# One channel group of the large convolution on GpSimd, 25 more table rows in the large projection, two items of the last stage at other places

## What is computed

```python
def conformer_conv(u, w_dw, b_dw, ln_g, ln_b):          # CONV_K = 31, CONV_W = 512
    a, gt = jnp.split(u, 2, axis=-1)
    h = a * jax.nn.sigmoid(gt)
    hp = jnp.pad(h, ((0, 0), (CONV_K - 1, 0), (0, 0)))
    h = lax.conv_general_dilated(hp, w_dw[:, None, :].astype(h.dtype), window_strides=(1,), padding='VALID',
                                 dimension_numbers=('NWC', 'WIO', 'NWC'), feature_group_count=CONV_W) + b_dw
    return jax.nn.silu(layer_norm(h, ln_g, ln_b))

def peer_ffn(x, w_q, sub_k1, sub_k2, u_tab, v_tab):
    ...
    top_s, top_j = lax.top_k(cand_s, PEER_TOPK)          # 8 heads x 16 experts for each token
    idx = jnp.take_along_axis(cand_i, top_j, axis=-1)
    g = jax.nn.softmax(top_s, axis=-1).astype(x.dtype)
    ...
    def one_chunk(args):                                 # 128 tokens
        xb, ib, gb = args
        act = jax.nn.gelu(jnp.einsum('cd,ced->ce', xb, u_tab[ib]), approximate=False)
        return jnp.einsum('ce,ced->cd', gb * act, v_tab[ib])
```

## Time and profile before

| what | us |
|---|---|
| median of 3 runs | 3703.0 (3701.9 to 3706.6) |
| the profiled execution, its own time | 3718.67 |
| its span | 3716.9 |
| large projection, in the trace | 500 to 843 |
| attention and merge of the 768 tokens | 843 to about 1760 |
| last stage: blocks of u | 1905 to 2893 |
| last stage: blocks of v | 2893 to 3604 |
| last table row | ends 3681 |

### The profile page before, as it was taken

The page is one execution under the profiler, slowest core; times in us unless marked ns, Lnnn a source line. Parts: engine busy times, 40 slices in busy tenths (PEclk is TensorE's granted clock), DMA queues, the critical chain, the costliest instruction groups (busy, mean ns, idle before and its releaser), DMA issues.

```text
span 3716.9 us, 40306 instructions
## 1 busy us (share of the span) xinstructions
PE 3175.3 (85%) x14137; PEld 1748.0 (47%) x14161; DVE 2672.2 (72%) x5156; ACT 836.4 (23%) x2013; POOL 1574.0 (42%) x1321
## 2 busy tenths in 40 slices
PE   7579889987888795884899899898999999889970
PEld 5458545755555563542444344444444444333430
DVE  5755449976777665867778896978947874545779
ACT  6334212122121121210110272653810000000000
POOL 5100001124655434434534343435425667777564
PEclk9779999997889797997999999999999999999995
DMA  8469434356878747985869889989899999999996
GB/s 279 139 235 368 184 130 136 109 162 226 280 269 281 264 169 249 380 319 205 318 265 365 298 303 364 326 323 342 307 387 362 384 379 347 325 342 358 407 410 256
DMA packets 313258, 1073.17 MB, mean 289 GB/s; under 512 B 36704, under 2 KB 62944, under 8 KB 309216
## 3 DMA queue, kind: packets, MB, share of 16 engines
q0 software_dynamic: 170704, 606.75, 45.1%
q1 hardware_dynamic: 101904, 363.16, 26.4%
q10 hardware_dynamic: 40448, 100.68, 7.5%
HBM read 931.52 MB, written 138.94 MB: 288 GB/s over the span
## 4 chain that ended last, share of the span: by engine, by line
PE 17%; DMA 14%; POOL 12%; DVE 5%; issue 4%; ACT 1%; DVEq 0%; ACTq 0%; POOLq 0%
PE ps L1781 13%; DMA rows<-v,expert_ids 6%; POOL rows L133 5%; POOL hidden_sums L1746 4%; POOL turned_rows L133 3%; DMA rows<-u,expert_ids 3%; DMA turned_rows<-u,expert_ids 1%; DMA h_side_kept<-mixer_state 1%; DMA turned_rows<-v,expert_ids 1%; DVE rows L162 1%; PE ps L107 1%; PE ps L109 1%; PE ps L108 1%; DVE row_sums L168 1%; DMA mixer_state<-u_t 1%
## 5 line engine op out<-in xcount | busy, mean ns | idle before, releaser
L133 POOL DMA_INDIRECT rows<-u,expert_ids x477 | 581.7, 1219 | 851.3 <-DVE hidden_sums L162 726.9
L1781 PE MATMUL ps<-turned_rows,mixer_state 128*128 128x512 f32 x2048 | 899.7, 598 | 7.3 <-DMA mixer_state<-u_t 6.6
L133 POOL DMA_INDIRECT rows<-v,expert_ids x527 | 609.6, 1157 | 673.3 <-DVE row_sums L168 513.7
L168 DVE SCALAR_TENSOR_TENSOR row_sums<-rows,hidden_sums,row_sums 128x1024 f32<-128x1024 f32 x518 | 654.4, 1282 | 253.7 <-DMA rows<-v,expert_ids 248.5
L1818 PE MATMUL ps<-shared_64k 128*128 128x512 f32 x1536 | 674.8, 602 | 41.1 <-DVE shared_64k L1945 41.0
L1781 PEld LDWEIGHTS ps<-turned_rows,mixer_state 128*128 128x128 f32 x2048 | 388.1, 192 | 479.4 <-issue 469.3
L1818 PEld LDWEIGHTS ps<-shared_64k 128*128 128x128 f32 x1536 | 295.2, 193 | 420.6 <-issue 420.6
L162 DVE CUSTOM_DVE_ANT_0 rows<-rows,x_first 128x1024 f32<-128x1024 f32 x256 | 305.8, 1221 | 47.1 <-DMA rows<-u,expert_ids 44.8
L107 PE MATMUL ps<-x_hi_t_b,shared_64k 128*128 128x384 f16 x912 | 312.4, 343 | 18.4 <-DMA shared_64k<-w_pairs_kept 17.6
L162 DVE CUSTOM_DVE_ANT_0 rows<-rows,branches 128x1024 f32<-128x1024 f32 x221 | 268.7, 1219 | 73.8 <-DMA rows<-u,expert_ids 71.4
L108 PE MATMUL ps<-x_lo_t_b,shared_64k 128*128 128x384 f16 x912 | 310.9, 341 | 0.0
(11 more groups left out here) (526 smaller groups left out, 4990.3 us busy)
## 6 DMA issues: line engine op xcount, KB each, us to landing
mixer_state<-u_t ACTq DMA_DIRECT2D x128, 512.0 KB, 6.9
shared_64k<-v SPq DMA_DIRECT2D x128, 512.0 KB, 7.2
rows<-strips SPq DMA_DIRECT2D x32, 768.0 KB, 7.1
h_kept<-branches ACTq DMA_DIRECT2D x32, 768.0 KB, 10.5
shared_64k<-weights_kept SPq DMA_DIRECT2D x32, 768.0 KB, 8.9
shared_64k<-h_kept SPq DMA_DIRECT2D x32, 768.0 KB, 12.9
shared_64k<-s_pairs_kept SPq DMA_DIRECT2D x32, 512.0 KB, 6.6
rows<-w_t SPq DMA_DIRECT2D x30, 512.0 KB, 5.6
```

Source lines behind the costliest of these rows:

```text
L133: nc.gpsimd.indirect_dma_start(row_tile(M, n), None, A["u" if r < NSEL else "v"], bass.IndirectOffsetOnAxis(ap=M["idx"][:, c, e:e + 1], ax ...
L168: nc.vector.scalar_tensor_tensor(acc[:, e % 2, :], src, hid[:, c % 2, e:e + 1], acc[:, e % 2, :], ALU.mult, ALU.add).then_inc(used, 1)
L1781: m = pe.matmul(ps[:, 4 + u % 4, 0:UT], uk[u % 4][:, k, :], x1t[:, k, :], start=k == 0, stop=k == KD - 1)
```

## The change

Five things are changed.

- In `project` with GB, `conv_inputs` (the four multiplications of line 548) stands between the choices of chunk 0 and chunk 1, and the six first table rows behind both.
- The convolution of channel group 3 goes to GpSimd: `pool_taps(k)`, one TENSOR_SCALAR for step 0, and for each of the 30 others a TENSOR_SCALAR (product into `tap_product`) and a TENSOR_TENSOR (sum), each waiting for the one before. VectorE keeps groups 0 to 2 (`dve_taps`). From step 10 on GpSimd gathers three table rows behind each step, 17 times. TensorE's mean and VectorE's centring wait for both (`tap`, `pool_tap`). The projection of the first 256 tokens is left as it is.
- `PROJ_ROWS` has 60 rows instead of 35: two behind every second step and in the nine calls after the steps. The later lists begin 25 rows later; by the multiples of 128, attention now has 263 rows instead of 257 and the merge 93 instead of 92, so the last stage begins at row 416 instead of 384 and the dense blocks at row 472 instead of 440. `NROW` stays 1152.
- The third weight group begins at block 96 instead of 86; chunk 3's choice is spread over blocks 78 to 92 instead of 82 to 105, its exponentials on ScalarE come at block 93 instead of 106; chunk 4's choice ends at 141 instead of 150.
- `dense_row` counts 2.2 rows for a block of v instead of 2.1. Of the tables only lines are shown.

```diff
-PROJ_ROWS = spans_of(0, [1] * 35)
+PROJ_ROWS = spans_of(0, [1] * 6 + [2] * 15 + [2] * 3 + [2] * 6 + [1] * 4 + [1] * 2)
...
-    tap = sem("conv_tap")
+    tap, pool_tap, pool_mul = sem("conv_tap"), sem("conv_tap_pool"), sem("conv_product_pool")
...
+    dve_taps = range(4) if g.first else range(3)
...
     @block.gpsimd
     def _(pool):
+        def pool_taps(k):
+            src, w = hc[:, 3, k:k + n], M["dw"][:, 3, k:k + 1]
+            if k == 0:
+                nc.gpsimd.tensor_scalar(cacc[:, 3, :], src, w, cv[:, 0, 3:4], ALU.mult, ALU.add).then_inc(pool_tap, 1)
+            else:
+                pool.wait_ge(pool_tap, k)
+                nc.gpsimd.tensor_scalar(M["tap_product"], src, w, None, ALU.mult).then_inc(pool_mul, 1)
+                pool.wait_ge(pool_mul, k)
+                nc.gpsimd.tensor_tensor(cacc[:, 3, :], cacc[:, 3, :], M["tap_product"], ALU.add).then_inc(pool_tap, 1)
+
...
         else:
             decay_low()
-            gather_rows(nc, pool, M, A, 0, R_PROJ + NR)
+            gather_rows(nc, pool, M, A, 0, NR)
+            pool.wait_ge(c_in, NCONST)
+            pool.wait_ge(h_done, 4)
+            at = NR
+            for k in range(CK):
+                pool_taps(k)
+                if k >= 10 and at < R_PROJ - 6:
+                    gather_rows(nc, pool, M, A, at, at + 3)
+                    at += 3
+            gather_rows(nc, pool, M, A, at, R_PROJ + NR)
...
-        pe.wait_ge(tap, 4 * CK)
+        pe.wait_ge(tap, len(dve_taps) * CK)
+        if not g.first:
+            pe.wait_ge(pool_tap, CK)
...
-        if not g.first:
+        def conv_inputs():
+            for gr in range(4):
+                dve.wait_ge(sig, gr + 1)
+                nc.vector.tensor_tensor(hc[:, gr, CK - 1:], QF[:, gr, :], KF[:, gr, :], ALU.mult).then_inc(h_done, 1)
+            dve.wait_ge(h_done, 4)
+
+        if g.first:
+            conv_inputs()
+        else:
             dve.wait_ge(iota_in, 16)
-            for i in range(2):
-                choose(nc, dve, M, S, M["sco"][i], i, i, 0, NT)
-        for _ in range(6):
-            rows()
-        for gr in range(4):
-            dve.wait_ge(sig, gr + 1)
-            nc.vector.tensor_tensor(hc[:, gr, CK - 1:], QF[:, gr, :], KF[:, gr, :], ALU.mult).then_inc(h_done, 1)
-        dve.wait_ge(h_done, 4)
+            choose(nc, dve, M, S, M["sco"][0], 0, 0, 0, NT)
+            conv_inputs()
+            choose(nc, dve, M, S, M["sco"][1], 1, 1, 0, NT)
+            for _ in range(6):
+                rows()
...
         def taps(a, b):
             for k in range(a, b):
-                for gr in range(4):
+                for gr in dve_taps:
...
-WINDOW_AT = [30, 58, 86]
+WINDOW_AT = [30, 58, 96]
 ROWS_U_BLOCK = 2.9
-ROWS_V_BLOCK = 2.1
-CHOICE_SPAN = {5: (0, 20), 6: (24, 47), 7: (52, 75), 3: (82, 105), 4: (112, 150)}
+ROWS_V_BLOCK = 2.2
+CHOICE_SPAN = {5: (0, 20), 6: (24, 47), 7: (52, 75), 3: (78, 92), 4: (112, 141)}
...
-EXP_BLOCK = {5: 21, 6: 48, 7: 76, 3: 106}
+EXP_BLOCK = {5: 21, 6: 48, 7: 76, 3: 93}
...
+        M["tap_product"] = None if g.first else s1("tap_product_", [P, n], F32)[:]
```

More of the change, by code:

```diff
@@ L559, in taps @@
                     else:
-                        dve.wait_ge(tap, 4 * k + gr - 3)
+                        dve.wait_ge(tap, len(dve_taps) * (k - 1) + gr + 1)
                         nc.vector.scalar_tensor_tensor(acc, src, w, acc, ALU.mult, ALU.add).then_inc(tap, 1)
@@ L624, in _ @@
             rows()
-        dve.wait_ge(tap, 4 * CK)
+        dve.wait_ge(tap, len(dve_taps) * CK)
+        if not g.first:
+            dve.wait_ge(pool_tap, CK)
         dve.wait_ge(mean_mm, 1)
```

## The result

The changed kernel takes 3758.6 us in the median of its runs (3746.7 to 3777.2), the kernel before 3704.8 (3702 to 3707): a ratio of 1.015, interval 1.0106 to 1.0194, or 54 us longer (38 to 72). Forecast were 40 us more and 3743, range 3702 to 3772. The profiled execution, 3746.7 (span 3744.9), is the shortest of its four, and that of before (3718.7) lies 14 us above its median, so the two traces differ by only 28 us. In later series before spread from 3684 to 3730. Totals are therefore compared by ratios of medians, and single stages by traces.

A forecast was written before the change was run, and what follows sets the result against it. No engine was taken to bound the whole, so edits were priced by stage: projection +58, attention and merge +5, last stage −23, sum +40 us. On the profiled 3718.7 that gives 3758.7, less 15.7 for the median: 3743 us, range 3702 to 3772.

The forecast's parts named there:

- What bounds the kernel: Whole kernel: no single engine; VectorE has about 18 us slack in the projection, DMA engines are full late in the last stage.
- Part 1: Projection: convolution inputs ahead of the second choice start that choice at 582.0, 12.9 us later, and convolution steps near 638.
- Steps 0 to 10 run beside the choice ... and cost nothing: Projection: GpSimd's first convolution steps run beside VectorE's choice, mostly one-input instructions, and take no time from VectorE.
- Parts 2 and 3: Projection: VectorE's own steps take 144 us, twelve GpSimd steps add 34 us by blocking; they end at 816.
- each GpSimd step is VectorE time too: Projection: GpSimd's elementwise instructions and VectorE's two-input ones go one after the other; 2.85 us per step, twelve steps.
- Part 4: Projection: TensorE's mean sum waits for GpSimd's step 30, queued with gathers; ready at 875 instead of 818, projection 58 us longer.
- six steps 18: Projection: GpSimd's steps 25 to 30, ahead of TensorE's mean sum, were counted as 18 us.
- Part 5: Attention and merge: 6 rows more in attention and 1 in merging cost 5 us, between 0 and 8.
- Part 6: Last stage: 32 rows fewer at 1.28 us give −41 us, stalls give back 18 (0 to 35): −23 us.
- Rival A: Projection: VectorE is not held by GpSimd to any extent that counts; total 3711 us, chance 0.17.
- Rival B: Last stage: a removed row is worth more than 1.28 us, at 2.30 each total 3692 us; chance 0.11.
- Rival C: Projection and last stage: product slow as the addition, slow gathers, second-half stall at full cost; 3771 us, chance 0.12.

The follow-up runs named there:

- the last experiment: Kernel before with 15 more rows within the convolution steps and chunk 3's choice two blocks earlier, nothing on GpSimd: ratio 0.9923, 3677.9 us.

## Why the prediction was near, point by point

**What bounds the kernel: right.** The slack of 18 us is the one that the last experiment fills. That the last stage is a matter of bytes was seen for its end only. Over the whole stage the rate is 351 to 356 GB/s in ten traces, whether 611, 617 or 628 MB are moved. But bytes are not all of it: the placements alone, with the bytes of before, lengthen the stage in the trace from 1776 to 1788 us.

**Part 1: right in size, and short of one thing.** The inputs take VectorE until 580.84, the second choice starts there (forecast 582.0). But its first row starts at 636.96, 19.5 later than in the earlier trace rows. "Steps 0 to 10 run beside the choice ... and cost nothing" is the step that failed: the choice lasts 56.1 us beside GpSimd and 48.0 with the same order and no step on GpSimd (582.80 to 630.78), 48.3 in before. Its one-input MAX8 go on undisturbed, 0.20 us each as in before; two-input instructions do not:

```profile
616.30 2.83 DVE L1517 TENSOR_TENSOR shared_64k<-shared_64k 128x2048 f32<-128x2048 f32 x1
619.21 1.88 DVE L1524 TENSOR_TENSOR shared_64k<-shared_64k 128x256 f32<-128x256 f32 x1
```

In before these two take 2.29 and 0.42 (there L1488 and L1495). So the steps began at 645.7 and not at 638. With no step on GpSimd and the inputs moved they begin at 638.4, 9.3 later than in before counted from the first choice: that part of the sum was right.

**Parts 2 and 3: the end was right by luck, since two errors cancel.** VectorE's steps end at 814.2, forecast 816. They last 168.6 us; 155.8 − 29 + 17 is 144 (15 rows did add 17.2 us in the last experiment), so eleven steps of GpSimd took 25 us, 2.2 each, not twelve times 2.85. The late start of 8 us made up for it. The product was sized wrongly both ways: it lasts 2.2 us and not 1.2, and holds VectorE for 0.7. So the step "each GpSimd step is VectorE time too" is right in full for the addition, and for a third of the product. In the rows above VectorE's instruction ends 0.8 us behind the addition (670.15 behind 669.34) and 0.8 behind the short product (662.25 behind 661.43), so both hold it to their end. Beside the long product it ends 1.7 us behind the product's start, as beside the short one, and half a microsecond ahead of its end. The Trainium skill (SBUF — State Buffer, section "SBUF: two separate sides") has the other engine blocked for the whole instruction. The addition and the short product agree, the product of 2.2 us does not. The Trainium skill's GPSIMD Engine Reference, section "Engine selection", calls one input roughly line-rate: 768 columns in 0.91 to 0.98 us agree for the form with two operations, 2.2 us for the form with one does not.

**Part 4: the mechanism right, its size short by 14.** TensorE waited where it was said and for the engine and the gathers that were named; the mean sum ended at 882.8, forecast 875. The term "six steps 18" is the mis-sized one: at 4.0 to 4.2 us they are 25. Another 6 us lie behind the mean sum (31.4 us to the attention's first matmul instead of 25.1), where one row more had been counted as about 1; TensorE's wait for the stage to begin (22.2, in before 17.4) is 5 of them. The remaining 2 or 3 us are spread over the other terms. So the projection is 72.6 longer instead of 58.

**Part 5: not decided.** From the projection's end to the first table block the traces of before and after take 1061 and 1062 us. But this stretch varies: eight traces with the rows of after take 1052 to 1083 (median 1061), four with the rows of before, one of them with one more, 1047 to 1061 (median 1055). The seven rows cost between nothing and a few microseconds; 5 is not refuted.

**Part 6: near by totals; the traces show more.** The placements cost 23 us (18 forecast). With 20 rows fewer, and 0.5 us in the projection, the time falls by 28: 1.4 us a row, where 1.28 was taken. By the same reckoning, the new placements kept, 32 rows make 1.4 each (9 − 23 − 30 = −44 us in the kernel without GpSimd's group). So by totals the last stage should be −32 × 1.4 + 23 = −22, forecast −23. The two profiled executions show −43, which is 20 more than the forecast and 2 beyond the −41 that part 6 allowed; with the second trace of after it is −35. In traces a row comes to 1.5 us (the placements alone against the kernel without GpSimd's group, 1788 and 1741) to 1.9 (before against the last experiment, 1776 and 1738). Traces with the rows and the weight group of before span 1762 to 1776 us in this stage, those with all of after's 1732 to 1743. Totals and traces thus differ by 13 to 21 us here. The only trace of before is an execution 14 us above its median, which may be part of it; the rest is open.

**The sum.** By totals 72.6 + 0 to 5 − 22 = +51 to +56, measured +54 (38 to 72), forecast +40. What was missing lies in part 4: GpSimd's six steps of 4.2 us and the longer wait for the next stage. **Rival A** is refuted: VectorE is held. **Rival B** decides from 1.97 us a row; it is 1.4 by totals and 1.5 to 1.9 by traces. **Rival C**'s condition, a product as slow as the addition, came true, and its 75 us for the projection were nearly met; its stall at full price was not.

## What to carry over

Before work is moved from VectorE to GpSimd, count what the receiver's instruction takes from the giver: here a step saved 0.94 us of VectorE and cost it 2.3. First fill the slack that the trace shows with work that no other engine waits for: 15 rows beside 18 us of idle time gave 28 us, where the change with a channel group on GpSimd, more rows and new placements lost 54. And a result that TensorE waits for does not belong in a queue whose gathers wait for VectorE's later rows: TensorE waited 55 us for it.

## What the runs showed of the hardware

- GpSimd's TENSOR_SCALAR on 128x768 with one operation took 2.20 to 2.22 us where nothing held it, with two operations (the second an addition of 0.0) 0.91 in the median of 30. Why is open.
- Of its 2.2 us such a product held a two-input instruction of VectorE for 0.7 us only, exactly as the short form did; a TENSOR_TENSOR of 1.8 us (2.0 where it had to wait for VectorE itself) held it for 1.6.
- The projection's length repeats to 0.6 us over kernels that share it, while whole executions of one kernel differ by 15 to 40 us.
